# Modulation sums of two feed-forwards: a sliding one-column stationary tile, rows in one 96x128 region and one transpose

## The reference, cut to what matters

```python
cs = jax.nn.silu(c)
for layer in range(DEPTH):
    mod = cs @ mod_w[layer] + mod_b[layer]        # 1024 x 6144: six rows of 1024
    sh1, sc1, g1, sh2, sc2, g2 = jnp.split(mod, 6, axis=-1)
    h = modulate(rms_norm(x, norm_g[layer, 0]), sh1, sc1)
    ...
    x = x + g1[:, None, :] * y
    h = modulate(rms_norm(x, norm_g[layer, 1]), sh2, sc2)
    x = x + g2[:, None, :] * conv_ffn(h, ...)     # hidden width 2816
```

## Time and profile before

| | us |
|---|---|
| median of 3 runs | 1572.47 (1569.87 to 1573.28) |
| the profiled execution | 1573.68 |
| its span | 1571.9 |
| TensorE matmuls busy | 1463.6 (93%) |
| VectorE busy | 1207.0 (77%) |
| ScalarE busy | 756.6 (48%) |
| TensorE's share of the chain that ended last | 71% |
| VectorE's share of that chain | 14% |

### The profile page before, as it was taken

The page is one execution under the profiler, slowest core; times in us unless marked ns, Lnnn a source line. Parts: engine busy times, 40 slices in busy tenths (PEclk is TensorE's granted clock), DMA queues, the critical chain, the costliest instruction groups (busy, mean ns, idle before and its releaser), DMA issues.

```text
span 1571.9 us, 26257 instructions
## 1 busy us (share of the span) xinstructions
PE 1463.6 (93%) x9806; PEld 1244.4 (79%) x9820; DVE 1207.0 (77%) x1895; ACT 756.6 (48%) x1080; POOL 51.5 (3%) x38
## 2 busy tenths in 40 slices
PE   5598989999999899999989889999999999999998
PEld 2484468999978666999979765689998787799997
DVE  7998747999989947799995557576667768776666
ACT  3322356444454525544436567565555632365544
POOL 2501100000000000000000100000000000000000
PEclk7798999999999989999998999999999999999999
DMA  9333836878846554988853510335455433354551
GB/s 363 136 109 127 328 148 248 341 295 316 335 162 270 214 196 179 391 331 317 336 194 124 162 40 1 116 141 212 169 182 199 164 118 134 115 175 172 183 197 69
DMA packets 57320, 314.72 MB, mean 200 GB/s; under 512 B 6902, under 2 KB 8159, under 8 KB 33119
## 3 DMA queue, kind: packets, MB, share of 16 engines
q1 hardware_dynamic: 53272, 302.40, 51.2%
q10 hardware_dynamic: 3974, 11.33, 2.2%
HBM read 310.98 MB, written 1.15 MB: 199 GB/s over the span
## 4 chain that ended last, share of the span: by engine, by line
PE 71%; DVE 14%; ACT 6%; issue 5%; DMA 3%; ACTq 0%; DVEq 0%; POOL 0%; SPq 0%
PE bank L2090 58%; DVE w_lo L1213 2%; PE bank L2335 2%; ACT w_hi L691 2%; DMA raw<-in_stream 1%; PE bank L2349 1%; PE bank L2370 1%; PE bank L1976 1%; DVE hf L1426 1%; DVE arena L1251 1%; PE bank L1994 1%; ACT arena L1007 1%; DVE x L1432 1%; ACT hf L1130 1%; PE bank L2158 1%
## 5 line engine op out<-in xcount | busy, mean ns | idle before, releaser
L2090 PE MATMUL bank<-h_hi,w_hi 128*128 128x256 f32 x1928 | 554.7, 288 | 17.2 <-DVE h_lo L1414 15.6
L2090 PE MATMUL bank<-h_lo,w_hi 128*128 128x256 f32 x1928 | 547.7, 284 | 0.0
L2090 PE MATMUL bank<-h_hi,w_lo 128*128 128x256 f32 x1928 | 547.6, 284 | 0.0
L1213 DVE TENSOR_TENSOR w_lo<-raw,w_hi 128x2048 fp32r<-128x2048 f32 x186 | 426.2, 2292 | 135.7 <-ACT w_hi L691 134.5
L691 ACT ACTIVATE w_hi<-raw 128x2048 fp32r<-128x2048 f32 x186 | 355.9, 1915 | 133.0 <-PE bank L2090 74.9
L2090 PEld LDWEIGHTS bank<-h_hi,w_hi 128*128 128x128 f32 x1928 | 372.0, 193 | 19.0 <-DVE h_lo L1414 9.6
L2090 PEld LDWEIGHTS bank<-h_lo,w_hi 128*128 128x128 f32 x1928 | 372.2, 193 | 2.1 <-issue 0.7
L2090 PEld LDWEIGHTS bank<-h_hi,w_lo 128*128 128x128 f32 x1928 | 372.1, 193 | 0.0
L1629 DVE SCALAR_TENSOR_TENSOR arena<-bank,par,arena 128x255 f32<-128x255 f32 (+1 forms) x264 | 109.1, 476 | 109.9 <-ACT arena L921 77.5
L2090 PE MATMUL bank<-w_hi,a_hi 128*128 128x512 f32 x368 | 145.9, 396 | 7.1 <-DVE a_lo L1654 6.2
L2090 PE MATMUL bank<-w_hi,a_lo 128*128 128x512 f32 x368 | 145.0, 394 | 0.0
(11 more groups left out here) (299 smaller groups left out, 1774.9 us busy)
## 6 DMA issues: line engine op xcount, KB each, us to landing
raw<-in_stream SPq DMA_DIRECT2D x186, 1024.0 KB, 4.9
arena<-in_mod_stream SPq DMA_DIRECT2D x64, 768.0 KB, 6.3
arena<-in_mod_later SPq DMA_DIRECT2D x48, 512.0 KB, 5.7
raw<-in_mod_pe SPq DMA_DIRECT2D x36, 512.0 KB, 6.2
arena<-in_mod_pe SPq DMA_DIRECT2D x12, 512.0 KB, 12.2
sq<-row_store ACTq DMA_DIRECT2D x7, 512.0 KB, 3.7
sq<-in_bias SPq DMA_DIRECT2D x8, 256.0 KB, 6.6
x<-in_x_t ACTq DMA_DIRECT2D x1, 1024.0 KB, 8.8
```

The lines of the kernel that those rows point to most:

```text
L1213: nc.vector.tensor_tensor(w_lo[s][:], raw[s][:], w_hi[s][:].bitcast(F32), ALU.subtract).then_inc(lo_done, 1)
L2090: ins = nc.tensor.matmul(out_, l, r, start=first and n == 0, stop=last and n == 2, **kw)
```

## The change

- `mod_block` no longer adds its two partial sums. Both go to TensorE, in both feed-forwards in the three `mod_acc` buffers; `mod_keep` and `mod_turn` are gone.
- `mod_sum` replaces `mod_turn_now`: six matmuls a block, the stationary side being a 128x32 window of a tile whose column 31 is ones and whose other 63 columns are zeros. The window that begins at 31 - b puts block b into row b of a region of 32 rows; three regions (partitions 0, 32, 64) take the three pieces of a block. All accumulate in bank 6 (96x128), which `open_mod` clears.
- Block 0 is summed on VectorE ahead of the loop, the three in the loop become blocks 3i+1, 3i+2, 3i+3, and none is left behind it. TensorE runs the sum of 3i after `up_gate` of the odd step, 3i+1 after its `down`, 3i+2 after `up_gate` of the even step, and block 15 behind the loop, ahead of `down(10)`.
- TensorE's loop of 5 turns is written out in these two feed-forwards; the other engines keep theirs.
- `rows_out` (VectorE, ahead of the `x_add`s) adds the bias as rows into `mod_rows` [96, P]; `columns_turn` (TensorE, after `down(10)`) transposes it once; `columns_out` (VectorE, after the `x_add`s) copies it into `mod`. `mod_out`, `rows_turn(1)` and `rows_turn(3)` go.
- `store_rows(1)` and `store_rows(3)` on ScalarE have no copy, and three DMAs instead of one. Two more small DMAs bring the one-column tile and the bias rows.

```diff
+    picks = np.zeros((2, P, 64 + P), np.float32)
+    picks[:, :, 31] = 1
...
+                if i % 2:
+                    act.wait_ge(sem("gates_known"), 3 + 2 * (i // 2))
+                    for g in range(3):
+                        act.dma_start(row_store[i, 0:n * P].rearrange("(b g p) -> g b p", g=3, p=P)[g], mod_rows[32 * g:32 * g + MOD_BLOCKS, :])\
+                            .then_inc(sem("row_stored"), 16)
+                    return
...
             store_rows(0)
+            act.dma_start(at(ARENA - 512, 64 + P), A["mod_pick"][0]).then_inc(sem("row_stored"), 16)
...
                 if p == 1:
                     store_rows(1)
+                    act.dma_start(row_bias, A["mod_pick"][1][:, 64:]).then_inc(sem("row_stored"), 16)
...
-                part = mod_acc[b % len(mod_acc)]
-                if b < MOD_BLOCKS:
-                    if b >= len(mod_acc):
-                        dve.wait_ge(sem("mod_turned"), b - len(mod_acc) + 1 + 3 * per)
-                    parts = [part[:, 0, :], part[:, 1, :]]
-                else:
-                    k0 = b % MOD_BLOCKS * MOD_COLS
-                    parts = [mod_keep[:, bass.ds(k0 + 3 * MOD_COLS * per, MOD_COLS)], part[:, 1, :]]
+                parts = [mod_acc[b % len(mod_acc)][:, e, :] for e in range(2)]
+                if b >= len(mod_acc):
+                    dve.wait_ge(sem("mod_turned"), b - len(mod_acc) + 1 + 3 * per)
...
-                    if kt == DT // 2 - 1:
+                    if kt % 4 == 3:
                         ins.then_inc(sem("mod_used"), 1)
...
-                chain_wait(last[1])
-                nc.vector.tensor_tensor(parts[0], parts[0], parts[1], ALU.add).then_inc(sem("mod_used"), 1)
...
+            def rows_out(r):
+                dve.wait_ge(sem("mod_turned"), MOD_BLOCKS * (r + 1))
+                dve.wait_ge(sem("row_stored"), ROW_STORED[2 * r])
+                nc.vector.tensor_tensor(mod_rows[:], bank[6][0:96, 0:P], row_bias[0:96, :], ALU.add).then_inc(sem("gates_known"), 1)
+
+            def columns_out(r):
+                dve.wait_ge(sem("rows_turned"), 2 * r + 2)
+                l = (1, 4)[r]
+                nc.vector.tensor_copy(mod[:, l, 0:48].rearrange("p (b g) -> p g b", g=3),
+                                      bank[7][:, 0:96].rearrange("p (g b) -> p g b", g=3)[:, :, 0:MOD_BLOCKS]).then_inc(sem("gates_known"), 1)
+                dve.wait_ge(sem("gates_known"), 4 + 2 * r)
...
+                if b0 is not None:
+                    mod_block(b0, c0)
...
-                    run(2 * i + 1, q0 + 2, q0 + 5, i, {0: 0, 2: 1})
-                    run(2 * i + 2, q0 + 5, q0 + 8, i, {0: 2})
+                    run(2 * i + 1, q0 + 2, q0 + 5, i, {0: 1, 2: 2})
+                    run(2 * i + 2, q0 + 5, q0 + 8, i, {0: 3})
...
                 if b0 is not None:
-                    mod_block(b0 + 15, c0)
+                    rows_out(f)
...
+            def open_mod(r):
+
+                pe.wait_ge(sem("row_stored"), ROW_STORED[0])
+                pe.wait_ge(sem("rows_copied"), r + 1)
+                nc.tensor.matmul(bank[6][:, 0:P], zeros[:, 0:P], zeros[:, 0:P], start=True, stop=False, skip_group_check=True)
+
+            def mod_sum(b, r):
+
+                pe.wait_ge(sem("mod_used"), MOD_SLOTS + 2 * (MOD_BLOCKS * r + b) + 2)
+                for e in range(2):
+                    for g in range(3):
+                        ins = nc.tensor.matmul(bank[6][32 * g:32 * g + 32, 0:P], pick[:, 31 - b:63 - b],
+                                               mod_acc[(MOD_BLOCKS * r + b) % len(mod_acc)][:, e, g * P:(g + 1) * P],
+                                               start=False, stop=b == MOD_BLOCKS - 1, skip_group_check=True)
                 ins.then_inc(sem("mod_turned"), 1)
+
+            def columns_turn(r):
+
+                pe.wait_ge(sem("gates_known"), 3 + 2 * r)
+                turn(bank[7][:, 0:96], mod_rows[:], 96).then_inc(sem("rows_turned"), 1)
...
+                        up_gate(s, q)
+                        mod_sum(3 * i + 2 * e, f)
+                        down(s - 1, q + 2)
+                        if not e:
+                            mod_sum(3 * i + 1, f)
+                else:
+                    for i in range(5):
+                        two_steps(i)
+                    mod_sum(MOD_BLOCKS - 1, f)
                 down(10, q0 + 32, last=True)
                 if b0 is not None:
-                    mod_turn_now(b0 + 15, 45)
+                    columns_turn(f)
...
-            ffn(1)
-            mod_turn(MB[4], range(0, 3))
+            ffn(1, MB[4])
...
-                    mod_turn(MB[4], range(3, 6))
-            mod_turn(MB[4], range(6, 11))
...
-                    mod_turn(MB[4], range(11, 14))
-            mod_turn(MB[4], range(14, 16))
```

More of the change, by code:

```diff
@@ L200, in laid_out @@
     out["rows"] = np.stack([w["cm_b_out"][0], w["final_g"], w["hy_b_out_2"][0], w["final_g_2"]])
+    picks = np.zeros((2, P, 64 + P), np.float32)
+    picks[:, :, 31] = 1
+    for i, n in enumerate(("mod_b", "mod_b_2")):
+        cols = w[n].reshape(-1, P)[48:].reshape(MOD_BLOCKS, 3, P)
+        for g in range(3):
+            picks[i, 32 * g:32 * g + MOD_BLOCKS, 64:] = cols[:, g]
+    out["mod_pick"] = picks
     out["ctx_t"] = tiled(w["ctx_2"][0].T).reshape(P, -1)
@@ L1700, in ffn @@
                     x_add(j, X_VERSION[(2, BOTH, 12, FINAL_2)[f]], t, fh, bank[j], 2 * f + 1)
+                if b0 is not None:
+                    columns_out(f)
             nc.vector.memset(both_wide, 0.0).then_inc(sem("both_zero"), 1)
@@ L2312, in ffn, with two_steps @@
                 first_up_gate(q0, h_of(FFN_NORM[f]))
+                if b0 is not None:
+                    open_mod(f)
                 if f == 2:
                     filter_layer(1)
-                with pe.Fori(0, 5) as i:
+                def two_steps(i):
                     for e in range(2):
                         s, q = 2 * i + 1 + e, q0 + 2 + 3 * e
-                        up_gate(s, q, i)
-                        if b0 is not None and e:
-                            mod_turn_now(b0 + 1, 9 * i + 3, i)
-                        down(s - 1, q + 2, i)
-                        if b0 is not None:
-                            mod_turn_now(b0 + 2 * e, 9 * i + 6 * e, i)
+                        if b0 is None:
+                            up_gate(s, q, i)
+                            down(s - 1, q + 2, i)
+                            continue
+                        q += 6 * i
+                        up_gate(s, q)
[3 more added lines that the diff above has]
+                            mod_sum(3 * i + 1, f)
+                if b0 is None:
+                    with pe.Fori(0, 5) as i:
+                        two_steps(i)
+                else:
+                    for i in range(5):
+                        two_steps(i)
+                    mod_sum(MOD_BLOCKS - 1, f)
                 down(10, q0 + 32, last=True)
                 if b0 is not None:
-                    mod_turn_now(b0 + 15, 45)
+                    columns_turn(f)
             ffn(0, MB[1])
@@ L2383, in _ @@
                 later(p)
-                if p == 0:
-                    rows_turn(1)
             conv_taps(3)
```

33 lines of the change are left out of this document (10 added, 23 removed).

## The result

The changed kernel takes 1580.21 us in the median of 15 runs (1577.83 to 1583.96). The kernel before, run beside it, takes 1572.47 (1568.21 to 1577.55). The ratio is 1.0054, with a 95% interval of 1.0044 to 1.0064. So it is slower by 8.5 us (7 to 10). I had forecast 1573.6 and no measurable change. The time lies just inside the range, at its top. I had given a slowdown of over 0.2% a chance of 0.35, and that is what came.

The account below looks back on a forecast made before the run. TensorE was taken as the bound, VectorE close behind. Feed-forward 0 -0.5, feed-forward 1 +5.8, behind it -4.0, transposes -0.2: +1.1 us, median 1572.47 to 1573.6; range 1567.0 to 1580.5.

Parts of the forecast that it names:

- The price of a sum: TensorE, both feed-forwards: 0.7 us a sum against 0.65 a turn; +1.4 us in feed-forward 0, +11.2 in feed-forward 1.
- Start of the loop: TensorE waits for VectorE's first blocks: +1.4 us in feed-forward 0, +4.0 in feed-forward 1; low clock behind, +0.7 and +2.2.
- B: Stretch from the start of feed-forward 0 to its `up_gate(2)`: forecast +2.9 us.
- F: Stretch from the start of feed-forward 1 to its `up_gate(2)`: forecast +7.6 us.
- End of the loop and its clock: Ahead of the last `down` of feed-forwards 0 and 1: waits shrink, -1.5 and -3.4 us; low clock goes, -1.4 and -1.5.
- Stretch D: Last `down` and tail of feed-forward 0, from `up_gate(10)` to `cm_in`: forecast -3.9 us.
- The tail of feed-forward 1: From the last matmul of `down(10)` to `dq`: 14.5 us would become 7.8, or -6.7.
- ScalarE and the queues: Extra stores and small loads: under 1.5 us more, hidden under other waits; +1 if that cover went.
- `dq` and `dkv`: Behind feed-forward 1: turns ahead of `dkv` go but it waits for norm 6, -2.1 us; together -4.0.
- The third group: The third group of turns, at `dkv` behind feed-forward 1, goes: -1.9 us.
- The written-out loop: TensorE's loops of feed-forwards 0 and 1: written-out code costs 0 us, bounds 0 and 3.
- Rival 1: Slower: the three strips overlap less in the sums, from 0.85 us a sum on, 1578.4 us or more; chance 0.35.

Follow-up runs that it names:

- e4_lag: Changed kernel with each sum one slot later on TensorE, blocks 14 and 15 both ahead of the last `down`: 1.0002 of the kernel before, 8.2 us less.
- e8_one_store: Changed kernel with each of the two row stores as one DMA of 96 rows instead of three of 16: 1.0042 of the kernel before.
- f2_awake: Changed kernel with zero matmuls where TensorE idles in the tail of feed-forward 1, ahead of `dkv` and behind it: 1.0036 of the kernel before.
- e3_late_lo: Changed kernel with VectorE's last loop turn written out and the last `lo` done behind the norm: 1.0032 of the kernel before, 3.5 us less.
- g4_all_awake_again: Repeat of the changed kernel with stores early, last `lo` late, sums one slot later and idle places filled with zero matmuls: 0.9966 of the kernel before.
- f4_two_steps: A kernel of the changed kind; the text tells neither what was changed in it nor its time.
- e5_all: Changed kernel with both stores early, last `lo` behind the norm and each sum one slot later: 0.9988 of the kernel before, 1571.1 us.
- e7_half_sums: Changed kernel with three matmuls a sum instead of six, half of the products left out: 1.0022 of the kernel before, 5.0 us less.
- e2_stores_early: Changed kernel with the two row stores moved to where ScalarE idles, ahead of the norms behind feed-forwards 0 and 1: 1.0038 of the kernel before.
- g1_looped: Changed kernel with TensorE's loop kept as a loop of five turns, modulation rows wrong: 1.0033 of the kernel before, beside 1.0053 for the unaltered changed kernel.

## Why the prediction was wrong

- **The price of a sum** was right in its slope (0.07 us a matmul, four strips' rows carried over to three) and 0.06 us short in its fixed part: +1.4 us over both feed-forwards, with the turn's 0.69 instead of 0.65. By the rule of the Trainium skill that I had set beside it (TensorE: Matmul & The Clock Gate, Measured speedup vs the span model: 2.38 times for three strips) three matmuls would take 0.27 us, an estimate. The trace does not agree: 0.207 were measured, as much as my 0.21 for a lone one, so here the strips overlap fully. The 0.8 us that I got from that rule is near 0.76 only by the fixed part.
- **Start of the loop.** The mechanism was right, and e4_lag shows it to be the dearest part of the change. The sizes were off both ways: without the sums B grew by 3.2 us, with the clock, where I had 2.1, and F by 2.8, where I had 6.2. The first is in part luck of the profile. In seven profiles TensorE and VectorE run the same instructions up to there, and the first wait in feed-forward 0 was 0.38 us (e8_one_store) to 2.26. It was short where ScalarE had the third chunk at 15.6 to 15.8 us after the start of feed-forward 0, and over 2 us where it had it at 17.2 to 17.5. In f2_awake the two waits were 0.61 and 1.37, close to my 0.5 and 1.65.
- **End of the loop and its clock.** Right. From `up_gate(10)` to the last matmul of `down(10)` feed-forward 1 went from 27.52 to 24.10 us with 1.5 us of sums added, 4.9 less by my count for the wait and the clock, which is the forecast's 3.4 and 1.5. Stretch D came out at -3.8 for -3.9, but from two misses that cancel: to the last matmul of `down(10)` it lost 2.3 us where I had 2.8, and behind it 1.5 where I had 1.1.
- **The tail of feed-forward 1: the failed step.** The forecast let the adds "follow `down` at once" and said that "VectorE's last three adds and columns come to the same" as TensorE's 3.5 us of zeros and transpose, and from that -6.7. It gave 1.8. The 4.9 us are three things, all in the rows above. Once block 15 was gone, the last `lo` took its place, and it waits for ScalarE: 1.9 us, by e3_late_lo. The four `x_add`s take 2.06 us each from the first bank on, while I had counted the operations of one as left behind `down`: 1.8 us, which stay in e3_late_lo and g4_all_awake_again (9.6 us to `dq`, not 7.8). And under this wait the clock fell as before the change, so that the transposes took 1.2 us more than I had counted.
- **ScalarE and the queues: the other failed step.** "Under which TensorE waits for a DMA or ScalarE for TensorE": costed at nothing, with 1 us if the cover went. The cover was not there: 1.0 us in `cm_in` and 0.7 in `uq`.
- **`dq` and `dkv`.** -1.7 for -2.1 in `dq`. The third group's 1.9 us was saved in `dkv` (from its start to the rotary matmul 25.2 us became 23.5), and went again in `uq`, 1.5 of it to the clock and 0.7 to the store. I had named a wait of about 3 us ahead of `dkv`, but costed neither hole, of 3.46 and 2.81 us, for its clock, though I had costed exactly this at the loops' start. The low level at `dkv`'s start was there before and changes nothing; the one in `uq` is new, in both profiles of this kernel.
- **The written-out loop** was taken as free with a bound of 3 us. Three of four pairs put it near that bound; it is not settled.
- **Rivals.** Rival 1, slower by the strips, had the right sign and the wrong mechanism. The slower side was made of a tail that gave 4.9 us less than I had booked, of stores at 1.7, a fall of the clock at 1.5, sums at 1.4 and the start of feed-forward 0 at 1.1, against which the start of feed-forward 1 gave 3.4 back. That is 7.2 us. I had +1.1 in all, and the medians moved by 7.7, the ratio by 8.5, so the miss is 6.6 to 7.4. It leaves little for the written-out loop, but each part is read from single profiles.
- **The range** held by luck. Its top stands for a sum of 0.9 us, and the sum is 0.76. By its own rate of 3.2 us for each 0.1 us that top would be 1580.0, and the measured 1580.21 is inside only because it was written as 1580.5.

## What to carry to other kernels

When work leaves an engine, look at what is next in that engine's own list before the gain is booked: here another `lo` and then four adds. When work leaves a place where TensorE waits, the wait stays and may bring the low clock with it, so that work which looked like pure cost was cheap; look at the clock there before the change too, since it may be low already. A sum that depends on another engine's block should be issued a slot later than the block is due: this alone was worth 8.2 us, and with the stores moved, the last `lo` behind the norm and the holes filled, the kernel takes 1567 to 1568 us, 0.9968 and 0.9966 of the kernel before (both intervals end at 0.9980), and so beats both.

## What the runs showed of the hardware that I had not expected

- In `cm_in` a DMA issue took 0.33 to 0.44 us of ScalarE's queue of instructions. In `uq`, right behind the two DMAs of the rotary copies, the same stores took 2.03, 2.43 and 0.84 us. In the kernel before the one store came there 2.9 us after the second of those DMAs and took 0.34. What holds the later ones up no run shows.

```profile
895.09 2.03 ACTq L750 DMA_DIRECT2D row_store<-mod_rows  x1
897.15 2.43 ACTq L750 DMA_DIRECT2D row_store<-mod_rows  x1
899.61 0.84 ACTq L750 DMA_DIRECT2D row_store<-mod_rows  x1
```

- The fall of the clock behind a wait is not settled by the wait's length. In feed-forward 0 it came behind 2.05 to 2.26 us in four profiles and not behind 2.06 in f4_two_steps. Ten profiles of the changed kind have the same waits of 3.46 us ahead of `dkv` and 2.8 behind it. In all ten the low level falls on the first matmuls of `dkv`; in three (e5_all, e7_half_sums, f4_two_steps) it lasts twice as long, in four (the changed kernel twice, e3_late_lo, e4_lag) it comes again behind the second wait, in three (e2_stores_early, e8_one_store, g1_looped) neither. The kernel before had it at `dkv` with no idle time at all. With every idle stretch from the tail to `uq` filled to under 0.75 us it did not come there in any of four profiles. It costs 1.3 to 1.5 us each time. Runs of one kernel differ by 6 to 13 us, and are mostly longer where the mean granted clock is lower (correlation -0.65, -0.64 and -0.67 in three sets of 35, 35 and 23 runs of the kernel before, but -0.19 in a fourth of 29).
